# Three norms around a two-block transformer kernel's feed-forwards: where the mean is taken, on what shape the root, and which engine multiplies

## The reference

```python
def rms_norm(x, g):
    y = x * rsqrt(mean(x * x, axis=-1) + EPS)
    return y * g

# first block, after the mixer: x = x + y @ w_out
h = rmsnorm(x, g_ffn)
gate = causal_dwconv3(h @ w_gate, ffn_conv_w, ffn_conv_b)
x = x + (silu(gate) * (h @ w_up)) @ w_down
# ... gated projection of p; then the second block
x = x + rms_norm(mix, norm_mix_post)                 # "post"
hn = rms_norm(x, norm_ffn_pre)                       # "ffn2"
ff = (gelu(dwconv3(hn @ w_gate)) * (hn @ w_up)) @ w_down
x = x + rms_norm(ff, norm_ffn_post)                  # "fpost"
```

## Time and profile before

| | before |
|---|---|
| median of three runs | 1533.25 us |
| lowest, highest | 1527.27, 1533.96 us |
| span of the profiled execution | 1531.9 us |
| its own time beside the span | not recorded |
| TensorE matmul busy | 1371.7 us, 90% |
| VectorE busy | 861.9 us, 56% |
| GpSimd busy | 848.0 us, 55% |
| ScalarE busy | 382.6 us, 25% |
| mean granted TensorE clock | 0.946 of 2.4 GHz |

### The profile page before, as it was taken

How to read it: one execution, slowest core, us unless ns; L and a number is a source line. 1 busy time by engine, 2 the same in 40 slices (tenths; PEclk the granted TensorE clock), 3 DMA queues, 4 the chain that set the end, 5 groups by cost and what they waited for, 6 DMA issues and landing times.

```text
span 1531.9 us, 18215 instructions
## 1 busy us (share of the span) xinstructions
PE 1371.7 (90%) x6036; PEld 1100.2 (72%) x6036; DVE 861.9 (56%) x1026; ACT 382.6 (25%) x709; POOL 848.0 (55%) x523
## 2 busy tenths in 40 slices
PE   5999987899999999999966765988969999999994
PEld 3777765678888888888755665755757888888883
DVE  6654454657666631239579988245457666662004
ACT  3123332112211110023444232334323221111001
POOL 5552332668666666677565432521285866666663
PEclk9999998899999999999978878996889999999997
DMA  6221120313222222332112000210021322222321
GB/s 242 80 72 55 42 69 7 104 69 110 97 96 98 82 99 95 115 105 94 69 42 69 14 28 28 72 42 14 14 97 55 110 96 96 96 81 84 101 77 55
DMA packets 35520, 117.59 MB, mean 77 GB/s; under 512 B 3952, under 2 KB 4336, under 8 KB 35344
## 3 DMA queue, kind: packets, MB, share of 16 engines
q1 hardware_dynamic: 34848, 115.18, 22.0%
q10 hardware_dynamic: 624, 1.77, 0.3%
HBM read 114.84 MB, written 2.10 MB: 76 GB/s over the span
## 4 chain that ended last, share of the span: by engine, by line
PE 75%; DVE 15%; issue 4%; ACT 3%; POOL 2%; DMA 0%; POOLq 0%; DVEq 0%; ACTq 0%
PE PS L461 23%; PE PS L463 22%; PE PS L462 22%; DVE KS L1642 3%; DVE QS L1641 2%; PE PS L564 2%; POOL WH L379 1%; PE PS L764 1%; PE PS L859 1%; DVE SA L1679 1%; PE PS L584 1%; DVE RS L1369 1%; DVE TMP L1676 1%; PE PS L844 1%; DVE ACC L1365 1%
## 5 line engine op out<-in xcount | busy, mean ns | idle before, releaser
L381 POOL TENSOR_TENSOR WL<-RAW,WH 128x1024 fp32r<-128x1024 f32 (+1 forms) x227 | 520.8, 2294 | 40.2 <-POOL WH L379 37.9
L379 POOL TENSOR_SCALAR WH<-RAW 128x1024 fp32r<-128x1024 f32 (+1 forms) x227 | 238.0, 1048 | 468.6 <-PE PS L463 461.1
L461 PE MATMUL PS<-AH,WH 128*128 128x512 f32 x928 | 374.0, 403 | 39.5 <-DVE AL L1355 17.6
L463 PE MATMUL PS<-AH,WL 128*128 128x512 f32 x928 | 365.7, 394 | 0.0
L462 PE MATMUL PS<-AL,WH 128*128 128x512 f32 x928 | 365.6, 394 | 0.0
L461 PEld LDWEIGHTS PS<-AH,WH 128*128 128x128 f32 x928 | 176.5, 190 | 96.8 <-issue 44.4
L463 PEld LDWEIGHTS PS<-AH,WL 128*128 128x128 f32 x928 | 176.7, 190 | 37.9
L462 PEld LDWEIGHTS PS<-AL,WH 128*128 128x128 f32 x928 | 176.8, 191 | 37.0 <-issue 1.9
L461 PE MATMUL PS<-SH,WH 128*128 128x512 f32 x352 | 136.9, 389 | 0.0
L462 PE MATMUL PS<-SL,WH 128*128 128x512 f32 x352 | 136.9, 389 | 0.0
L463 PE MATMUL PS<-SH,WL 128*128 128x512 f32 x352 | 136.9, 389 | 0.0
(11 more groups left out here) (282 smaller groups left out, 2061.6 us busy)
## 6 DMA issues: line engine op xcount, KB each, us to landing
RAW<-in_w SPq DMA_DIRECT2D x163, 512.0 KB, 3.2
RAW<-in_w SPq DMA_DIRECT2D x32, 384.0 KB, 3.0
RAW<-in_w SPq DMA_DIRECT2D x32, 320.0 KB, 2.8
X<-in_x SPq DMA_DIRECT2D x4, 512.0 KB, 7.5
BT<-in_bias SPq DMA_DIRECT2D x1, 2048.0 KB, 14.4
out<-X SPq DMA_DIRECT2D x8, 256.0 KB, 2.2
PIN<-in_p ACTq DMA_DIRECT2D x1, 512.0 KB, 3.9
LM<-in_masks ACTq DMA_DIRECT2D x1, 512.0 KB, 3.3
```

What stands on the lines that cost most here:

```text
L379: nc.gpsimd.tensor_scalar(WH[:, slot, 0:width], RAW[:, slot, 0:width], 1.0, 1.0, ALU.mult, ALU.mult).then_inc(s_hi, 1)
L381: nc.gpsimd.tensor_tensor(WL[:, slot, 0:width], RAW[:, slot, 0:width], WH[:, slot, 0:width].bitcast(F32), ALU.subtract).then_inc(s_split, 1)
L461: nc.tensor.matmul(o, lh, rh, start=start, stop=False)
L463: return nc.tensor.matmul(o, ll, rh, start=False, stop=stop)
```

## The change

The mean ahead of the eighth tile goes ahead of the third tile, in both feed-forwards (`side_by_side` in `ffn`). For "post" and "fpost" the mean is taken as four columns of one number for each token, tokens on partitions (`root_of_columns`); root (`column_root`) and reciprocal (`column_reciprocal`) work on 128x4; TensorE turns the columns back into 128 equal rows by a product of the broadcast column with the identity, and VectorE copies these from PSUM to RS. The eight products MIX times RS of "post" go from GpSimd to VectorE, each linked to the addition behind it.

```diff
@@ tiles and semaphores
+        RT = COL[:, 248:252]
+        s_rt, s_rb = sem("s_rt"), sem("s_rb")
@@ gpsimd
-            over_rms("post", MIX, s_mix, range(DK))
             each_unit(pool, split, UNITS["ffn2"][0] + NS, NU)
             over_rms("fpost", MIX2, s_mix2, range(OWN, DK))
@@ tensor
+            def root_of_columns(n, count):
+
+                ge(pe, s_acc[n], DK)
+                for t in range(NT):
+                    ins = nc.tensor.matmul(pb[7][:, t:t + 1], ACC[:, tokens(t)], INVD[:, 0:1], start=True, stop=True)
+                ins.then_inc(s_ms[n].sem, 1)
+                pe.wait_ge(s_rt, count)
+                for t in range(NT):
+                    ins = nc.tensor.matmul(pb[6][:, tokens(t)], RT[:, t:t + 1].to_broadcast([P, P]), IDENT,
+                                           start=True, stop=True)
+                ins.then_inc(s_rb, 1)
...
-                side_by_side(u0, range(4), AH, AL, s_gl[norm], {DK - 1: lambda: statistic(norm)})
+                side_by_side(u0, range(4), AH, AL, s_gl[norm], {2: lambda: statistic(norm)})
...
-            statistic("post")
-            ge(pe, s_sd["post"], 1)
+            root_of_columns("post", 1)
+            ge(pe, s_rs["post"], 1)
             ffn("ffn2", "ffn2", "down2", s_mix2)
-            statistic("fpost")
+            root_of_columns("fpost", 2)
@@ scalar
+            def column_root(n):
+                ge(act, s_ms[n], 1)
+                A(RT, pb[7][:, 0:NT], ACT.Sqrt, bias=EPS_C).then_inc(s_sd[n].sem, 1)
...
-            norm_root("post")
+            column_root("post")
...
-            norm_root("fpost")
+            column_root("fpost")
@@ vector
+            def column_reciprocal(n, count):
+                ge(dve, s_sd[n], 1)
+                V_.reciprocal(RT, RT).then_inc(s_rt, 1)
+                dve.wait_ge(s_rb, count)
+                V_.tensor_copy(RS[:], pb[6]).then_inc(s_rs[n].sem, 1)
+                ge(dve, s_rs[n], 1)
...
-            norm_reciprocal("post")
+            column_reciprocal("post", 1)
             for m in range(DK):
-                dve.wait_ge(s_mn, m + 1)
+                dve.wait_ge(s_mix, m + 1)
+                link(V_.tensor_tensor(MIX[:, m, :], MIX[:, m, :], RS[:], ALU.mult))
                 V_.tensor_tensor(X[:, m, :], X[:, m, :], MIX[:, m, :], ALU.add).then_inc(s_x["ffn2"].sem, 1)
...
-            norm_reciprocal("fpost")
+            column_reciprocal("fpost", 2)
...
-                    dve.wait_ge(s_mn, DK + m - OWN + 1)
+                    dve.wait_ge(s_mn, m - OWN + 1)
```

## The result

The changed kernel has a median of 1540.34 us over 19 runs (1533.82 to 1542.77); the kernel before, measured again beside it, 1533.57 (1526.68 to 1536.32). The ratio is 1.0046 with a 95% interval of 1.0032 to 1.006: 6.8 us slower, clear of no change by the interval, and inside the 0.5% that I had called the same. Predicted were 1539.0 and 1532 to 1545.

The account below looks back on a forecast made before the run. TensorE, 90% busy, was taken to bound the kernel, so edits count by its next matmul. Port 0.25, second-entry stall 7.1 and tail -1.5 gave +5.85 us on 1533.25: 1539.1, rounded to 1539.0, range 1532 to 1545.

Parts of the forecast that it names:

- What bounds: Whole kernel: TensorE 90% busy; at both feed-forward resumptions gate product and weight unit 5's split end within 0.01 us.
- Part 1: First feed-forward, mean before the third tile: gain 0, since the split does not move; perhaps a 0.25 us loss.
- Rival B: Both feed-forward entries: gate product alone held TensorE, each gains 2.13 us; total +1.1, 1534.3 us; chance 0.12.
- The charge of 0.25 for the port: Feed-forward entries: GpSimd's split loses 0.25 us to VectorE's step on their shared SBUF port, bounds 0 and 0.7.
- Part 2: Post norm by four columns: roots stand 3.76 us behind the last square, 1.5 us sooner, bounds 0.9 and 2.0.
- Part 5: Tail: root and reciprocal, 4.06 us, replaced by 2.54; gain 1.5 us, bounds 1.1 and 1.9.
- Part 3: Second feed-forward entry, products on VectorE: 2.58 us per tile, TensorE starts 4.6 us earlier, squares end at T + 20.2.
- Part 4: Second feed-forward, mean before the third tile: TensorE stalls 9.2 us for eight squares, resumption 7.1 us later.
- The sum: Whole kernel: 0.25 + 7.1 - 1.5 = +5.85 us.
- Rival C: Low clock weighs more: long slow stretch after the stall, another after the first entry, slow way back; +8.7, 1542.0 us; chance 0.22.
- D: The forecast itself, whole kernel: +5.85 us, bounds of about 2 us; chance 0.63.
- Rival A: Second feed-forward: squares are there by the third tile, no stall; whole kernel -12.0, 1521.2 us; chance 0.03.

Follow-up runs that it names:

- mean_first_only: Kernel before with the mean moved ahead of the third tile in the first feed-forward only; 1534.5 us, ratio 0.9994.
- columns_only: Kernel before with both norms (post, fpost) by four columns, products left on GpSimd, means ahead of the eighth tile; 1533.57 us, ratio 0.9995.
- mean_back_second: Changed kernel with the second feed-forward's mean put back ahead of the eighth tile; 1528.88 us, ratio to before 0.996.
- mean_seventh: Changed kernel with the second feed-forward's mean ahead of the seventh tile; 1529.65 us, ratio to before 0.9985.
- banks_in_turn: Changed kernel, both feed-forward entries finishing their last tiles bank by bank, second mean ahead of the seventh tile; 1520.59 us, ratio to before 0.9919.
- turn_everywhere: banks_in_turn with both output projections also finishing their last tiles bank by bank; 1512.71 us, ratio to before 0.9861.
- products_only: Kernel before with the eight products of post moved to VectorE and nothing else; 1532.93 us, ratio 0.9997.
- turn_only: Kernel before with feed-forward entries finishing bank by bank, means ahead of third (first) and seventh tile (second); 1530.2 us, ratio 0.996.

## Why the prediction was right, point by point

**What bounds.** That two chains end together at the resumption was the reading on which part 1 rested. It is shown: with the mean early the idle time stays (2.06, 2.05, 2.04 us) and only the releaser's name changes, and with the slot released early it goes. Rival B falls. The tie is looser than I worked out, though. From the split's end to TensorE's start I took 0.24 us, read ahead of the first matmul of the entry. At the resumption it was 0.13 or 0.14 where the split released TensorE: 322.84 to 322.98 in mean_first_only, 1173.74 to 1173.87 after the change. Before, the split alone would have let TensorE start at about 323.10, 0.1 us ahead of the gate product's 323.21 and not 0.01, and the idle stretch lost just that, from 2.13 to 2.05.

**Part 1.** No gain from the first mean: the idle stretch stays, and the ratio is 0.9994 for it alone. The charge of 0.25 for the port was wrong at both entries: the split's second half took 2.34 and 2.35 us, where it had taken 2.35 before with no such VectorE step beside it, and VectorE's step lost the whole meeting. The timeline of VectorE after has it, beside GpSimd's half from 1171.39 to 1173.74:

```profile
1171.47 2.81 DVE L1539 SCALAR_TENSOR_TENSOR TMP<-PAD,PRM,TMP 128x512 f32<-128x512 f32 x1 [0.28 <-ACT TMP L1089]
```

The rule of the Trainium skill that I set beside it ("SBUF — State Buffer", Who interferes with whom), a whole instruction is locked out and whoever starts first keeps the port, agrees with this row; my reading of it, that GpSimd might be the loser here, did not.

**Part 2.** Roots 4.19 us behind the last square, worked out 3.76. The term that was mis-sized is the way back: eight passes took 1.79 us, not 1.3. I had put it between the two clocks; it ran at a granted clock of 0.60. **Part 5** failed by the same term: gain 0.56, not 1.5, which is below the lower bound of 1.1. There the way back took 2.08, at a granted clock of 0.50, and the one-column means 1.31 instead of 1.05. The trace after is the slowest of six here: in the five runs with the same tail (columns_only, mean_back_second, mean_seventh, banks_in_turn, turn_everywhere) the distance was 4.13 to 4.38 us, a gain of 1.0 to 1.2.

**Part 3.** The first matmul came 1135.39 - 1131.81 = 3.58 us behind the roots (3.52 worked out), the sum of squares 20.12 behind them (20.2), 2.59 a tile (2.58). Alone, the products gain 3.6 us. Part of it is that the two engines no longer hinder each other: before, as long as GpSimd multiplied, to 1149.36, VectorE's additions took 1.5 to 1.8 us each, and 0.68 from then on the earlier trace rows. GpSimd and VectorE before:

```profile
1137.05 12.31 POOL L451 TENSOR_TENSOR MIX<-MIX,RS 128x512 f32<-128x512 f32 x8 [3.17 <-DVE RS L1369]
```
```profile
1144.76 1.76 DVE L1806 TENSOR_TENSOR X<-X,MIX 128x512 f32<-128x512 f32 x1
```

**Part 4.** The stall was 8.77 us (9.2 worked out; the two tiles ahead of it took 7.82 to their end and not 7.48). From the mean's start to the resumption 21.89 us, worked out 1.12 + 13.6 + 2.4 + 4.88 + 0.25 = 22.25. The half clock took the mean (2.07 instead of 1.02) and the seven matmuls behind it; from the mean's start to that of the last tile, at 1168.94, it was 16.96 us, where I had 17.12. From there to the resumption it was 4.93 and not 5.13. The stage grew by 7.06 us (7.1 predicted). That it fits so well is partly luck: the roots came 0.43 us later than worked out, and the smaller errors behind them, the port's among them, took 0.5 back.

**The sum.** In the traces second entry +7.06 and tail -0.56. The first entry was 1.1 us shorter to the resumption, for the slow stretch at its start was, and 1.6 longer behind it, where the clock now fell (0.50 from 324.5 to 327.4). Sum +7.0 against +5.85 worked out and 6.8 measured. But these two terms are not shown to be the change's: they stand in the traces of columns_only and products_only too, whose first mean is not moved, and neither stands in that of mean_first_only, where it is. The difference of the medians is therefore not explained to the last microsecond. Rival C had three terms. Its slow stretch after the first entry came in this trace (1.6), and its way back near half clock came in both norms (0.5 and 0.8 us above my 1.3); the long slow stretch behind the stall did not, as the mean itself ran at half clock and the slow matmuls behind it were correspondingly fewer. What kept the sum near D was this and the errors the other way, at the first entry and the port. Rival A, that the squares are there in time, is refuted by the 8.77 us.

## What to carry to other kernels

Before a reduction is moved ahead in an in-order stream, compare two paces: when its last input is ready, and when the engine would get there. Where the input is later, everything behind the wait pays. When a wait that the profile names is taken away, look for the second condition of the same instruction; here the split behind a weight slot that came free late ended within some 0.1 us of it. Finishing side-by-side accumulators one after another over the last tiles releases the first operand early. With the earlier means it gave 0.4% on the kernel before (turn_only), where the first mean's move alone had given nothing. On the change it took the ratio from 0.9985 (mean_seventh) to 0.9919, and with the projections to 0.9861. The best of the norm edits without it, mean_back_second, gave 0.4%.

## What the runs showed of the hardware that I had not expected

The fp32 mean of 512 columns took 1.02 us in the midst of matmuls, 1.12 after 1.9 us of idleness and 2.07 after 8.8 us; the matmuls behind the latter were slow only until 1156.84, 4.9 us after the stall's end. After a wait of 2.04 to 2.13 us at the resumption the clock fell in some traces and stayed in others, at the same place of the program: the first twelve matmuls behind the first entry's wait took 4.44 us after the change and 2.84 in mean_first_only. The eight 128x128 fp32 passes of the way back, behind half a microsecond of waiting, took between 1.67 and 2.08 us in the traces taken, never the 0.90 that I had as the bound of full clock. And the mixer's stretch from 980 to 1060 us ran at granted clocks from 0.83 (turn_only) to 0.94 (after), though no edit touches it. Between the traces before and after this hid 4.4 of the 6.8 us by which the medians differ. What decides that clock is left open; no run was made for it.
